# Two x tiles loaded and turned ahead of the last modulation sums, and the first projection reordered

## What is computed

```python
c_act = jax.nn.silu(c)
mod = (c_act @ w_ada[l] + b_ada[l])[:, None, :]
sh1, sc1, gt1, sh2, sc2, gt2 = jnp.split(mod, N_MOD, axis=-1)
h = rmsnorm(x, g_mix[l]) * (1.0 + sc1) + sh1
proj = h @ w_in[l]
```

## Time and profile before

| | |
|---|---|
| median of three runs | 1037.28 us (1036.64 to 1039.13) |
| profiled execution, its own time | 1039.98 us |
| profiled execution, span | 1038.2 us |
| PE busy | 992.2 us, 96% of the span |
| DVE busy | 676.5 us, 65% |
| ACT busy | 447.7 us, 43% |
| POOL busy | 410.0 us, 39% |
| chain that ended last | PE 78%, DVE 11%, ACT 3%, issue 2%, POOL 2%, DMA 2%, SP's queue 2% |

### The profile page before, as it was taken

One profiled execution on the slowest core, in us unless ns is written; L12 is line 12 of the kernel. 1 busy time (PEld: TensorE's weight loads), 2 busy tenths in 40 slices (PEclk: granted clock), 3 DMA queues, 4 the chain that ended last, 5 costly groups with the idle time before them and its releaser, 6 DMA issues.

```text
span 1038.2 us, 12646 instructions
## 1 busy us (share of the span) xinstructions
PE 992.2 (96%) x4605; PEld 815.9 (79%) x4605; DVE 676.5 (65%) x957; ACT 447.7 (43%) x759; POOL 410.0 (39%) x306
## 2 busy tenths in 40 slices
PE   5799989999999999989999999999999999999995
PEld 0598877788888887868888888888888888888884
DVE  5848865767524589956746745844846864747867
ACT  0663246867621466532333333333234442634442
POOL 1313666499603121054643643644642300037510
PEclk9699999999899999989999999999999999999998
DMA  9902110544113333356356255255357998755513
GB/s 325 362 1 102 42 41 1 175 131 127 55 53 111 102 122 101 113 177 207 112 170 205 102 180 186 104 180 182 125 159 261 340 353 312 253 200 172 196 71 153
DMA packets 119929, 165.20 MB, mean 159 GB/s; under 512 B 8694, under 2 KB 61754, under 8 KB 119868
## 3 DMA queue, kind: packets, MB, share of 16 engines
q1 hardware_dynamic: 119868, 164.40, 47.1%
HBM read 124.26 MB, written 40.11 MB: 158 GB/s over the span
## 4 chain that ended last, share of the span: by engine, by line
PE 78%; DVE 11%; ACT 3%; issue 2%; POOL 2%; DMA 2%; SPq 2%; DVEq 0%; POOLq 0%; ACTq 0%
PE PS L2137 39%; PE PS L2171 16%; PE PS L1841 14%; PE PS L1900 4%; PE PS L2015 3%; DMA ADA<-in_w_ada 1%; PE PS L2027 1%; DVE GT L1301 1%; DVE RS L1277 1%; POOL ropeQ L731 1%; ACT PR L986 1%; DVE RT L1273 1%; PE PS L2087 1%; POOL WIN L714 1%; DVE XD L1815 1%
## 5 line engine op out<-in xcount | busy, mean ns | idle before, releaser
L2171 PE MATMUL PS<-RE 128*128 128x512 f32 x924 | 210.5, 390 | 0.0
L2171 PEld LDWEIGHTS PS<-RE 128*128 128x128 f32 x924 | 173.5, 188 | 36.7 <-ACT DU L1217 0.4
L1313 DVE TENSOR_TENSOR RE<-REraw,RE 128x1024 fp32r<-128x1024 f32 x77 | 107.0, 1426 | 73.8 <-ACT RE L1149 73.0
L2137 PE MATMUL PS<-HT,WS 128*128 128x512 f32 x528 | 125.9, 395 | 4.6 <-ACT U L1132 4.6
L1149 ACT ACTIVATE RE<-REraw 128x1024 fp32r<-128x1024 f32 x77 | 81.4, 1061 | 103.3 <-DMA REraw<-t_scratch 67.9
L2137 PE MATMUL PS<-HB,WS 128*128 128x512 f32 x528 | 123.3, 389 | 0.0
L2137 PEld LDWEIGHTS PS<-HT,WS 128*128 128x128 f32 x528 | 100.9, 191 | 26.2 <-issue 5.0
L2137 PEld LDWEIGHTS PS<-HB,WS 128*128 128x128 f32 x528 | 99.2, 188 | 20.5
L2137 PE MATMUL PS<-HT,W 128*128 128x512 f32 x480 | 110.8, 390 | 0.0
L2137 PEld LDWEIGHTS PS<-HT,W 128*128 128x128 f32 x480 | 90.0, 188 | 18.6
L1691 DVE TENSOR_TENSOR SG<-PS,PV 128x512 f32<-128x512 f32 x22 | 15.1, 684 | 106.7 <-PE PS L2137 106.7
(11 more groups left out here) (261 smaller groups left out, 1874.2 us busy)
## 6 DMA issues: line engine op xcount, KB each, us to landing
REraw<-h_scratch SPq DMA_DIRECT2D x77, 256.0 KB, 4.9
h_scratch<-SG SPq DMA_DIRECT2D x55, 256.0 KB, 2.4
ADA<-in_w_ada SPq DMA_DIRECT2D x12, 1024.0 KB, 8.2
TW<-in_w_down SPq DMA_DIRECT2D x22, 512.0 KB, 4.4
t_scratch<-TW SPq DMA_DIRECT2D x44, 256.0 KB, 5.0
REraw<-t_scratch SPq DMA_DIRECT2D x44, 256.0 KB, 5.1
REraw<-in_w_down SPq DMA_DIRECT2D x33, 256.0 KB, 6.5
X<-in_x SPq DMA_DIRECT2D x16, 512.0 KB, 9.3
```

The costliest lines, as they stand in the source:

```text
L1313: dve.tensor_tensor(out_, full, hi.bitcast(F32), ALU.subtract).then_inc(ready, 1)
L2137: ins = pe.matmul(PS[:, bank, :], l, r, start=fresh and z == 0, stop=z == len(terms) - 1, skip_group_check=not fresh)
L2171: ins = pe.matmul(PS[:, D_BASE[p] + j, :], RE[e][:, a, 0, tok(j)], RE[e][:, b, 1, :], start=p in (1, 2, 7) and i == 0 and x_ == 0, stop=i ...
```

## The change

The loads of x 0 and x 1 go ahead of sh1 2, and `WTMraw` ahead of x 2 and x 3. ACT sums the squares of tiles 0 and 1 ahead of the copy to `SHROW`, and those of tiles 2 to 7 in pairs behind `modulate1(0)`, `(1)` and `(2)`. DVE runs `roots1(0)` between `accumulate(1)` and `accumulate(2)`, the copy `COLS` ahead of `accumulate(3)`, and `MOD` and `G1` right behind `accumulate(3)`; then three low parts of `WTM`, `h_lo(0)`, the fourth, and only then `roots1(2)`. PE turns tiles 0 and 1 ahead of `col_sum(0)`; behind `col_sum(1)` stand sixteen new transposes of `IDENT` into a PSUM bank that nothing reads; tile 2 is turned behind the projection of tile 0, and tiles 3 to 7 in the middle (behind k = 3) of the projections of tiles 1 to 5.

```diff
@@ SP
         load_sh1(1)
         load_ada(1)
+        load_x(0)
+        load_x(1)
         load_sh1(2)
         load_ada(2)
         load_sh1(3)
-        load_x(0)
         load_ada(3)
-        for t in range(1, 4):
-            load_x(t)
         for i in range(4):
             sp.dma_start(WTMraw[:, 2 * i:2 * i + 2, :], win_d[:, 2 * i:2 * i + 2, 0:TM]).then_inc(wtm_in[i], 16)
-        for t in range(4, NT):
+        for t in range(2, NT):
             load_x(t)
@@ ACT
         squares1(0)
+        squares1(1)
 
         act.wait_ge(S["sh1_rows"], 1)
         act.activation(SHROW[0:1], PS[0:1, 4:6, :], ACT.Copy).then_inc(S["sh1_out"], 1)
-        for t in range(1, 4):
-            squares1(t)
         for t in range(NT):
             modulate1(t)
-            if t < 4:
-                squares1(t + 4)
+            if t < 3:
+                squares1(2 * t + 2)
+                squares1(2 * t + 3)
             if t >= 3:
                 tm_out(t - 3)
@@ DVE
-        for j in range(1, 4):
-            accumulate(j)
-        dve.wait_ge(S["rowsT"], 1)
-        dve.tensor_copy(COLS[:], PS[:, 6, 0:N_ROWS])
...
+        accumulate(1)
         roots1(0)
+        accumulate(2)
+        dve.wait_ge(S["rowsT"], 1)
+        dve.tensor_copy(COLS[:], PS[:, 6, 0:N_ROWS])
+        accumulate(3)
...
         for i in range(4):
-            if i == 1:
-                roots1(2)
-            if i == 2:
+            if i == 3:
                 h_lo(0)
             dve.wait_ge(S["wtm_hi"], i + 1)
...
+        roots1(2)
         for t in range(1, NT):
@@ PE
-        col_sum(0)
-
-        pe.wait_ge(S["sh1_out"], 1)
-        for k in range(KT):
-            ins = pe.matmul(PS[:, 7, k:k + 1], SHROW[...], ONES[0:1, 0:1], start=True, stop=True)
-        ins.then_inc(S["sh1_sum"], 1)
-        col_sum(1)
...
         turn_x1(0)
         turn_x1(1)
-        for t in range(NT):
-            if t < NT - 2:
-                turn_x1(t + 2)
-            pe.wait_ge(S["h_ready"], t + 1)
...
+        col_sum(0)
+
+        pe.wait_ge(S["sh1_out"], 1)
...
+        col_sum(1)
+
+        for _ in range(16):
+            pe.transpose(PS[:, 5, 0:P], IDENT[:], IDENT[:])
+
+        def project(t, k0, k1):
...
+        project(0, 0, KT)
+        turn_x1(2)
+        for t in range(1, NT):
+            project(t, 0, 4)
+            if t < NT - 2:
+                turn_x1(t + 2)
+            project(t, 4, KT)
```

More of the change, by code:

```diff
@@ L1869, in _ @@
         ins.then_inc(S["sh1_rows"], 1)
-        col_sum(0)
-        pe.wait_ge(S["sh1_out"], 1)
-        for k in range(KT):
-            ins = pe.matmul(PS[:, 7, k:k + 1], SHROW[0:1, k // 4, (k % 4) * P:(k % 4 + 1) * P], ONES[0:1, 0:1], start=True, stop=True)
-        ins.then_inc(S["sh1_sum"], 1)
-        col_sum(1)
         def turn_x1(t):
@@ L1889, in _ @@
         turn_x1(1)
-        for t in range(NT):
-            if t < NT - 2:
-                turn_x1(t + 2)
-            pe.wait_ge(S["h_ready"], t + 1)
-            if t >= 2:
-                pe.wait_ge(S["tm_out"], t - 1)
-            for k in range(KT):
+        col_sum(0)
+        pe.wait_ge(S["sh1_out"], 1)
+        for k in range(KT):
+            ins = pe.matmul(PS[:, 7, k:k + 1], SHROW[0:1, k // 4, (k % 4) * P:(k % 4 + 1) * P], ONES[0:1, 0:1], start=True, stop=True)
+        ins.then_inc(S["sh1_sum"], 1)
+        col_sum(1)
+        for _ in range(16):
+            pe.transpose(PS[:, 5, 0:P], IDENT[:], IDENT[:])
+        def project(t, k0, k1):
+            if k0 == 0:
+                pe.wait_ge(S["h_ready"], t + 1)
+                if t >= 2:
+                    pe.wait_ge(S["tm_out"], t - 1)
+            for k in range(k0, k1):
                 if t == 0 and k % 2 == 0:
@@ L1900, in _ @@
                     ins = pe.matmul(PS[:, 4 + t % 2, 0:TM], HT[:, a, k, tok(t)], WTM[:, b, k, :],
-                                    start=(k == 0 and p == 0), stop=(k == KT - 1 and p == 2))
-            ins.then_inc(S["tm_done"], 1)
+                                    start=(k == 0 and p == 0), stop=(k == KT - 1 and p == 2), skip_group_check=True)
+            if k1 == KT:
+                ins.then_inc(S["tm_done"], 1)
+        project(0, 0, KT)
[5 more added lines that the diff above has]
+            project(t, 4, KT)
         def pool_group(i):
```

## The result

The changed kernel takes 1049.7 us (median of five runs, 1049.42 to 1050.45) against 1037.78 us before (median of five as well). The ratio is 1.0115, with a 95% interval of 1.0101 to 1.0128. The forecast was 1037.2, and the measured time lies far outside its range. The profiled execution has a span of 1048.2 us, against 1038.2.

What follows compares the result with a forecast made beforehand. PE was taken to set the time to about 113 us, then the DVE and POOL list to 145. PE's 2.3 us lead was lost there: 1037.28 + 0.1 - 0.2 (clock) = 1037.2 us, range with rivals 1034.0 to 1039.2.

Steps and rivals of the forecast that it cites:

- The turns in the tiles: Projections of tiles: turns still take 0.87 us, helpers ready 1 to 2 us ahead; PE ends 2.3 us earlier, at 89.8.
- Rival 2: PE rests 3.8 us ahead of 130.67, so the fourth WU group starts at half clock; 1038.6 us, chance 0.15.
- rival 3: Half clock at 31 us delays the columns to 42.3 and the list by 3.7 to 5; 1041 to 1042, chance 0.07.
- The loads, the front and the first projection: First 52 us: sh1's last piece at 27.6, modulate1(0) at 38.6, first projection 2.45 us earlier at 43.95, second at 51.4.
- the bound: accumulate(3) on DVE: 3.1 us from 30.3, plus 2.8 for three steps blocked by POOL's conversions, ending at 36.2.
- What the lead is worth: Behind tile 7: DVE's list shifts +0.1 us, POOL holds accumulate(6), PE's lead becomes a 3.8 us wait; +0.1 at 145.
- the forecast's own range: Whole kernel: the no-change forecast of 1037.2 us, chance 0.55, with its own range of 1035.9 to 1038.4.
- Rival 1: PE's lead is kept, at accumulate(6) or tile 7's early turn: 1034.1 to 1035.9 us, chance 0.23; 0.11 over 3.1 us.
- The clock's half: First projection: full clock expected a little more often than before, counted as -0.2 us in the total.
- Rival 2's cover: At 145.25, 2.08 us of PE waiting hides all but 0.4 of the 2.5 us that half clock costs.

Runs made afterwards that it cites:

- the run with the take-away edit: Changed kernel with ACT's take-away of tile t - 3's projection ahead of tile t's modulation, for tiles 3 to 7; 1038.81 us, ratio 1.0018 to the kernel before.
- with both: Changed kernel with ACT's take-away ahead of the modulation and tile t + 2 turned ahead of tile t's projection; 1036.71 us, ratio 0.9993 to the kernel before.
- the run with the turn a quarter in: Changed kernel with tile t + 2 turned behind six matmuls of tile t's projection, not twelve; 1043.17 us, ratio 1.0044 to the kernel before.

## Why the prediction was wrong

**The step that failed** stands under "The turns in the tiles": that from tile 2 on ACT, POOL and DVE are ready 1 to 2 us ahead. I had followed only the chain to `h_ready`. The projection of tile t also waits for the take-away of tile t - 2, and that stands in ACT's program behind the modulation of tile t + 1, whose turn had just been moved half a projection back. The text said that the move gives "half a tile less notice", and did not ask who uses that notice up. The notice was 4.87 + 0.87 = 5.74 us against a chain of 4.4 (2.75, 1.2 and the hand-overs), a slack of 1.3, which the trace of before shows (64.41 to 65.85, less a hand-over of 0.15). The move took 3.3: half a projection and the next turn. That leaves 2.0 a tile missing, four times, and with the first, larger wait (3.8) and the half clock behind it (1.6) 13.4 us, less the lead of 3.7: 9.7, where PE is 9.8 late. No rival held it: both rivals on the slower side, 2 and 3, were about the clock alone.

**The loads, the front and the first projection** were right in kind and too dear by up to 1.5 us. sh1's last piece was used at 27.23 (forecast 27.6). The small sums ran at full clock throughout, so `modulate1(0)` started at 37.18 (38.6, best case 37.5), the first projection at 42.52 (43.95) and the second at 49.84 (51.4; the best case was 50.5). `accumulate(3)` took 4.21 beside POOL's conversions, and not the 5.9 of the bound. Half clock at 31 us (rival 3) did not occur.

**What the lead is worth** was right, and it is the part that carries over. It was not tested by the change itself, whose lead was gone by tile 2, but by the run with the take-away edit. The prediction had DVE's list follow the turn of tile 7, `accumulate(6)` reach POOL's window sum just after that has started, and PE's lead end as a longer wait ahead of the column sum. That run, with a lead of 2.6 us for the 2.3 of the forecast, shows this nearly to the tenth: 81.54 for 81.8, 116.25 for 116.5, a wait of 4.06 for 3.8, and 145.21 for 145.3. Its median is still 1.9 us above before, outside the +1.1 of the forecast's own range, and that part was not explained. With the ring, the same list hands the loss through in full. Rival 1, PE's lead kept, is contradicted by the same rows.

**The rule on the shared port** (the Trainium skill, SBUF — State Buffer, "Who interferes with whom") agrees with these runs. DVE's four steps took 7.36, 8.83 and 7.94 us when they met POOL's window sums, and 3.1 us when moved away from them on the kernel before. The sooner DVE came behind the start of POOL's second window sum, the longer it was held, and it ended 9.0 us behind that start each time: 116.14 to 125.14 before, 126.51 to 135.51 changed, and 116.09 to 125.08 with the take-away edit, where POOL's row is

```profile
116.09 1.89 POOL L713 TENSOR_TENSOR WIN<-WIN 128x1024 f32<-128x1024 f32 x1
```

**The clock's half.** The 0.2 us given to the sixteen transposes were not there. The group behind PE's wait for the column sum took 13.1 us in the changed kernel instead of 11.5, at a granted clock of 0.69 from 141 to 145, and as long with the take-away edit and with both. But the wait's length does not decide it by itself: it was 2.10, 4.06 and 1.95 us in these three and 2.09 in the run with the turn a quarter in, whose group took 11.5. Rival 2's cover held: PE's wait at the product with `WUQ` shrank from 2.08 to 0.46 in exchange.

## What to carry to other kernels

When a step on one engine is moved back, go through every wait of the steps around it, the ones on free buffers too, and write down the ring that each closes: its length against the period of the bound engine is the slack, and moving one member by more than that costs the difference on every round. Where two engines' orders close a ring, exchanging two neighbours in either order can open it. And before giving an engine a lead, find the list that the next stage really waits for; here it had 10 us of DVE work that could stand in idle time.

## What the runs showed of the hardware

DVE and POOL held each other up: the four DVE steps that take 3.1 us alone took 7.36 to 8.83 beside POOL's window sums, and two of these sums took 5.11 us instead of 3.87. The delay grew with DVE's earliness, so that an earlier start gave nothing (116.25 + 8.83 and 117.78 + 7.36 both end at 125.1). Sixteen 128 by 128 transposes ahead of a projection did not make its clock full (0.51 from 44 to 47 us in the changed kernel). Transposes in the middle of an open accumulation cost no more than elsewhere: with the take-away edit it is 5.72 us from the turn at 59.16 inside one projection to the next at 64.88, and before it is 5.73 between turns that stand between projections (59.33 and 65.06). And the length of a half-clock stretch around small matmuls differs between executions of one kernel: the attention stage took 101.1 and 102.7 us in two executions of the kernel before.
